# Stick-breaking attention: how the loads of a head are shaped, queued and ordered

## The reference

```python
logits = einsum("bhqd,bhkd->bhqk", q, k) * scale
log_keep = where(visible, log_sigmoid(-logits), 0.0)
log_between = cumsum(log_keep, axis=3, reverse=True) - log_keep
weights = where(visible, exp(log_sigmoid(logits) + log_between), 0.0)
out = einsum("bhqk,bhkd->bhqd", weights, v)
```

## Time and profile before

| | us |
|---|---|
| median of 3 runs | 4376.24 |
| profiled execution, its own time | 4379.16 |
| its span, first to last instruction | 4377.4 |
| PE busy in the span | 4171.0 (95%) |
| DVE busy | 2380.5 (54%) |
| DVE waiting for a gate in the attention, 8 times | 61.2 |

### The profile page before, as it was taken

The page is one execution under the profiler, slowest core; times in us unless marked ns, Lnnn a source line. Parts: engine busy times, 40 slices in busy tenths (PEclk is TensorE's granted clock), DMA queues, the critical chain, the costliest instruction groups (busy, mean ns, idle before and its releaser), DMA issues. The chain is left out here.

```text
span 4377.4 us, 90822 instructions
## 1 busy us (share of the span) xinstructions
PE 4171.0 (95%) x35784; PEld 3344.7 (76%) x35784; DVE 2380.5 (54%) x3103; ACT 1666.2 (38%) x3296; POOL 804.4 (18%) x637
## 2 busy tenths in 40 slices
PE   7999999997999999997999999999899999999999
PEld 7888888985888888885555555655688888878887
DVE  5444444443444444442777777777467766743222
ACT  4222222223222222222666666666444444421111
POOL 2110111111111111110000000000256666610222
PEclk9999999998999999998999999999899999999999
DMA  2333433333333333334443442442233333355653
GB/s 93 109 117 119 122 109 110 102 115 110 109 118 116 109 104 118 107 103 113 89 94 69 82 93 63 87 94 62 75 114 99 101 104 100 92 184 177 189 188 129
DMA packets 486971, 479.74 MB, mean 110 GB/s; under 512 B 260610, under 2 KB 370818, under 8 KB 480914
## 3 DMA queue, kind: packets, MB, share of 16 engines
q1 hardware_dynamic: 475154, 450.33, 37.1%
q10 hardware_dynamic: 11520, 25.17, 1.6%
HBM read 305.45 MB, written 169.93 MB: 109 GB/s over the span
## 5 line engine op out<-in xcount | busy, mean ns | idle before, releaser
L1210 DVE TENSOR_TENSOR_SCAN kept<-keep,kept 128x512 f32<-128x512 f32 (+1 forms) x448 | 436.6, 975 | 63.1 <-ACT keep L1172 22.6
L1172 ACT ACTIVATE keep<-z 128x512 f32<-128x512 f32 (+3 forms) x704 | 343.4, 506 | 302.4 <-PE z L1105 242.1
L1636 POOL TENSOR_TENSOR off<-NT,tri 128x512 f32<-128x512 f32 x165 | 206.1, 1276 | 1181.6 <-ACT NT L1540 1181.6
L1115 PE MATMUL turned<-t_identity,kept 128*128 128x128 f32 (+1 forms) x2432 | 383.0, 280 | 38.6 <-DVE kept L1210 38.6
L1115 PEld LDWEIGHTS turned<-t_identity,kept 128*128 128x128 f32 (+1 forms) x2432 | 280.7, 136 | 154.9 <-DVE kept L1210 50.0
L1182 ACT COPY w<-turned 128x512 f32<-128x512 f32 (+4 forms) x704 | 363.2, 528 | 92.4 <-PE turned L1115 90.7
L1207 DVE TENSOR_TENSOR_SCAN kept<-keep,hidden 128x512 f32<-128x512 f32 (+3 forms) x256 | 284.2, 1116 | 156.3 <-ACT keep L1172 155.7
L1104 PE MATMUL z<-k_high,q_parts 128*128 128x512 f32 (+3 forms) x704 | 308.6, 439 | 36.1 <-DMA k_low<-scr_k_lo 27.9
L1142 PE MATMUL acc<-w,dv 128*64 128x512 f32 (+3 forms) x1280 | 322.8, 562 | 15.4 <-issue 15.4
L1104 PEld LDWEIGHTS z<-k_high,q_parts 128*128 128x128 f32 x704 | 137.8, 196 | 191.5 <-ACT keep L1172 107.6
L1105 PE MATMUL z<-k_low,q_parts 128*128 128x512 f32 (+3 forms) x704 | 256.6, 368 | 0.0
(11 more groups left out here) (554 smaller groups left out, 10688.4 us busy)
## 6 DMA issues: line engine op xcount, KB each, us to landing
w_raw0A<-in_w_main SPq DMA_DIRECT2D x42, 512.0 KB, 3.9
w_raw0B<-in_w_main SPq DMA_DIRECT2D x42, 512.0 KB, 3.9
w_raw1A<-in_w_main SPq DMA_DIRECT2D x41, 512.0 KB, 4.0
w_raw1B<-in_w_main SPq DMA_DIRECT2D x41, 512.0 KB, 3.8
KB<-scr_kb SPq DMA_DIRECT2D x33, 512.0 KB, 5.2
AR<-scr_ar SPq DMA_DIRECT2D x33, 512.0 KB, 5.4
y_raw<-scr_y SPq DMA_DIRECT2D x64, 256.0 KB, 4.5
merge<-scr_merge SPq DMA_DIRECT2D x64, 256.0 KB, 6.3
```

The lines of the kernel that those rows point to most:

```text
L1115: mm = pe.transpose(turned[num % TB][0:size, P * r:P * r + P], kept[kept_in(g)][:, src:src + size], t["identity"][:, :])
L1172: act.activation(keep[num % KB][:, 0:size], z[num % ZB][:, 0:size], ACT.Sigmoid, scale=-DH ** -0.5).then_inc(keep_done, 1)
L1210: dve.tensor_tensor_scan(dst, data, data, kept[kept_in(g)][:, end:end + 1], ALU.mult, ALU.bypass).then_inc(scanned, 1)
L1636: pool.tensor_tensor(out, a, b, op).then_inc(s[name], 1)
```

## The change

Five things are done, all in `attention_phase`.

1. `dv_diag` is loaded over all 128 rows by SP. The edge rows then go into row 127 on top of it, from POOL's queue, after a wait for the landing (`diag_in`, `diag_first`).
2. The load of a head is cut into five kinds (queries, high keys, low keys, steps, diagonal), which `due_after` spreads: odd head: queries at turn 7 of the pair before (for head 1: at turn 0), high keys at turn 0, low keys and steps at turn 1, diagonal at turn 2; even head of the next pair: queries and high keys at turn 3, low keys and steps at turn 4, diagonal at turn 5.
3. The four key loads are issued high, high, low, low instead of high, low, high, low.
4. At the start the constant `hidden` is loaded behind the first part's queries and keys instead of ahead of them, and the first two gates after the first of three parts instead of after the third.
5. PE waits for `v_in` (now 32 for each load) and for the edge rows (`edge_in`, 16).

```diff
+        def due_after(g):
+            pair, turn = divmod(g, 2 * GROUPS)
+            even, odd = 2 * pair + 2, 2 * pair + 1
+            if g == 0:
+                return [(odd, "queries"), (odd, "high")]
+            plan = {0: [(odd, "high")], 1: [(odd, "low"), (odd, "steps")], 2: [(odd, "diagonal")],
+                    3: [(even, "queries"), (even, "high")], 4: [(even, "low"), (even, "steps")], 5: [(even, "diagonal")],
+                    7: [(odd + 2, "queries")]}
+            return [(head, what) for head, what in plan.get(turn, []) if head < HEADS]
...
-            def load(head, first, last, qk_sem, v_sem):
...
-                for part in (low, high):
-                    sp.dma_start(k_high[u][part, ks].bitcast(F32), scratch["k_hi"][rows, src]).then_inc(qk_sem, 16)
-                    sp.dma_start(k_low[u][part, ks].bitcast(F32), scratch["k_lo"][rows, src]).then_inc(qk_sem, 16)
...
-                sp.dma_start(dv_diag[u][0:P - 1, tiles, :], by_tile[0:P - 1, tiles, :]).then_inc(v_sem, 16)
-                sp.dma_start(dv_diag[u][P - 1:P, tiles, :], edge[:, tiles, :]).then_inc(v_sem, 16)
...
+            def load_keys(head, first, last, dst, name, done):
...
+                for part in (slice(0, DH), slice(DH, P)):
+                    sp.dma_start(dst[u][part, ks].bitcast(F32), scratch[name][rows, src]).then_inc(done, 16)
...
+            def load_diagonal(head, first, last, done):
+                u, rows, tiles = head % 2, slice(DH * head, DH * head + DH), slice(first, last)
+                by_tile = scratch["dv"][CHUNK:TOK, rows].rearrange("(k p) c -> p k c", p=P)
+                sp.dma_start(dv_diag[u][:, tiles, :], by_tile[:, tiles, :]).then_inc(done, 16)
...
-            sp.dma_start(hidden[:, :], io["hidden"]).then_inc(const_in, 16)
             for p, (first, last) in enumerate(FIRST_PARTS):
-                load(0, first, last, qk_first[p], v_first[p])
-            load_gate(0)
-            load_gate(1)
+                load_queries(0, first, last, qk_first[p])
+                load_keys(0, first, last, k_high, "k_hi", qk_first[p])
+                load_keys(0, first, last, k_low, "k_lo", qk_first[p])
+                if p == 0:
+                    sp.dma_start(hidden[:, :], io["hidden"]).then_inc(const_in, 16)
+                load_steps(0, first, last, v_first[p])
+                load_diagonal(0, first, last, diag_first[p])
+                if p == 0:
+                    load_gate(0)
+                    load_gate(1)
             for g in range(GROUPS_ALL):
                 sp.wait_ge(y_done, g + 1)
                 store_y(g)
                 if g + 2 < GROUPS_ALL:
                     load_gate(g + 2)
-                if g % (2 * GROUPS) == 0:
-                    head = head_of(g) + 1
-                    load(head, 0, QT, qk_in[head % 2], v_in[head % 2])
-                if g % (2 * GROUPS) == GROUPS - 1 and head_of(g) + 2 < HEADS:
-                    head = head_of(g) + 2
-                    load(head, 0, QT, qk_in[head % 2], v_in[head % 2])
+                for head, what in due_after(g):
...
             def value_steps(g):
                 head = head_of(g)
                 if head == 0:
-                    pe.wait_ge(v_first[min(rank(g), len(FIRST_PARTS) - 1)], 64 if rank(g) == 0 else 48)
+                    pe.wait_ge(v_first[min(rank(g), len(FIRST_PARTS) - 1)], 32 if rank(g) == 0 else 16)
+                    pe.wait_ge(edge_first[min(rank(g), len(FIRST_PARTS) - 1)], 16)
                 else:
-                    pe.wait_ge(v_in[head % 2], 64 * loads_of(head))
+                    pe.wait_ge(v_in[head % 2], 32 * loads_of(head))
+                    pe.wait_ge(edge_in[head % 2], 16 * loads_of(head))
...
+            def load_edges(head, first, last, done):
+                edge = scratch["v_edge"][:, DH * head:DH * head + DH].rearrange("(o k) c -> o k c", o=1)
+                pool.dma_start(dv_diag[head % 2][P - 1:P, first:last, :], edge[:, first:last, :]).then_inc(done, 16)
+
+            for p, (first, last) in enumerate(FIRST_PARTS):
+                pool.wait_ge(diag_first[p], 16)
+                load_edges(0, first, last, edge_first[p])
+            for head in range(1, HEADS):
+                pool.wait_ge(diag_in[head % 2], 16 * ((head + 1) // 2 if head % 2 else head // 2))
+                load_edges(head, 0, QT, edge_in[head % 2])
```

More of the change, by code:

```diff
@@ L987, in attention_phase @@
         qk_first, v_first = [[sem(f"a_{x}_first{b}") for b in range(len(FIRST_PARTS))] for x in ("qk", "v")]
+        edge_first, edge_in = [sem(f"a_edge_first{b}") for b in range(len(FIRST_PARTS))], [sem(f"a_edge_in{b}") for b in range(2)]
+        diag_first, diag_in = [sem(f"a_diag_first{b}") for b in range(len(FIRST_PARTS))], [sem(f"a_diag_in{b}") for b in range(2)]
         qk_in, v_in = [sem(f"a_qk_in{b}") for b in range(2)], [sem(f"a_v_in{b}") for b in range(2)]
@@ L1026, in _, with load_queries @@
         @block.sync
         def _(sp):
-            def load(head, first, last, qk_sem, v_sem):
[L1029 to L1032, removed]
+            def load_queries(head, first, last, done):
+                u, rows, qs = head % 2, slice(DH * head, DH * head + DH), slice(P * first, P * last)
+                sp.dma_start(q_parts[u][0:DH, qs].bitcast(F32), scratch["q_hi"][rows, qs]).then_inc(done, 16)
+                sp.dma_start(q_parts[u][DH:P, qs].bitcast(F32), scratch["q_lo"][rows, qs]).then_inc(done, 16)
@@ L1033, in load @@
+            def load_keys(head, first, last, dst, name, done):
+                u, rows = head % 2, slice(DH * head, DH * head + DH)
                 k0 = P * first + (META if first else 0)
                 ks, src = slice(k0, P * last + META), slice(PAD + k0, PAD + P * last + META)
-                sp.dma_start(q_parts[u][low, qs].bitcast(F32), scratch["q_hi"][rows, qs]).then_inc(qk_sem, 16)
-                sp.dma_start(q_parts[u][high, qs].bitcast(F32), scratch["q_lo"][rows, qs]).then_inc(qk_sem, 16)
@@ L1037, in load, with load_steps @@
-                for part in (low, high):
-                    sp.dma_start(k_high[u][part, ks].bitcast(F32), scratch["k_hi"][rows, src]).then_inc(qk_sem, 16)
-                    sp.dma_start(k_low[u][part, ks].bitcast(F32), scratch["k_lo"][rows, src]).then_inc(qk_sem, 16)
-                tiles = slice(first, last)
+                for part in (slice(0, DH), slice(DH, P)):
+                    sp.dma_start(dst[u][part, ks].bitcast(F32), scratch[name][rows, src]).then_inc(done, 16)
+            def load_steps(head, first, last, done):
+                u, rows, tiles = head % 2, slice(DH * head, DH * head + DH), slice(first, last)
@@ L1041, in load @@
                 by_tile = scratch["dv"][CHUNK:TOK, rows].rearrange("(k p) c -> p k c", p=P)
-                edge = scratch["v_edge"][:, rows].rearrange("(o k) c -> o k c", o=1)
                 if first == 0:
                     sp.wait_ge(cleared, 2)
-                    sp.dma_start(dv[u][0:META, 0, :], scratch["dv"][PAD:CHUNK, rows]).then_inc(v_sem, 16)
-                sp.dma_start(dv[u][:, first + 1:last + 1, :], by_tile[:, tiles, :]).then_inc(v_sem, 16)
-                sp.dma_start(dv_diag[u][0:P - 1, tiles, :], by_tile[0:P - 1, tiles, :]).then_inc(v_sem, 16)
@@ L1048, in load @@
-                sp.dma_start(dv_diag[u][P - 1:P, tiles, :], edge[:, tiles, :]).then_inc(v_sem, 16)
+                    sp.dma_start(dv[u][0:META, 0, :], scratch["dv"][PAD:CHUNK, rows]).then_inc(done, 16)
+                sp.dma_start(dv[u][:, first + 1:last + 1, :], by_tile[:, tiles, :]).then_inc(done, 16)
+            def load_diagonal(head, first, last, done):
+                u, rows, tiles = head % 2, slice(DH * head, DH * head + DH), slice(first, last)
+                by_tile = scratch["dv"][CHUNK:TOK, rows].rearrange("(k p) c -> p k c", p=P)
+                sp.dma_start(dv_diag[u][:, tiles, :], by_tile[:, tiles, :]).then_inc(done, 16)
@@ L1067, in _ @@
                     load_gate(g + 2)
-                if g % (2 * GROUPS) == 0:
-                    head = head_of(g) + 1
-                    load(head, 0, QT, qk_in[head % 2], v_in[head % 2])
-                if g % (2 * GROUPS) == GROUPS - 1 and head_of(g) + 2 < HEADS:
-                    head = head_of(g) + 2
-                    load(head, 0, QT, qk_in[head % 2], v_in[head % 2])
+                for head, what in due_after(g):
+                    qk, v = qk_in[head % 2], v_in[head % 2]
+                    if what == "queries":
+                        load_queries(head, 0, QT, qk)
+                    elif what == "high":
+                        load_keys(head, 0, QT, k_high, "k_hi", qk)
+                    elif what == "low":
+                        load_keys(head, 0, QT, k_low, "k_lo", qk)
+                    elif what == "steps":
+                        load_steps(head, 0, QT, v)
+                    else:
+                        load_diagonal(head, 0, QT, diag_in[head % 2])
             for b in range(2):
```

## The result

The changed kernel takes 4301.76 us, the median of 4 runs (4298.37 to 4304.05), against 4376.98 us before (4 runs). The ratio is 0.9827, 95% interval 0.981 to 0.9844: 1.7% faster. The forecast was 4300. Measured once more with five runs beside two of the experiments it was 4303.18, ratio 0.9832 (0.9818 to 0.9845).

The account below looks back on a forecast made before the run. The prediction took SP, stopped by a diagonal load on one DMA engine, to bound the kernel. Seven stretches (57 us) and the start (20 us) gave 77 us off 4379.2, so 4302, named 4300 against the median; range 4285 to 4328.

Parts of the forecast that it names:

- The bound: Even-head loads: the 127-row diagonal on one DMA engine holds SP some 32 us, so gates and edges come late.
- One sign: In the changed profile of the attention, SP would never be held over 1 us by a DMA issue.
- The seven stretches: Sum 6 to sum 8 in seven head pairs: DVE-bound, 16.9 us instead of 25.04 each, 57 us in all.
- The start: Start of attention: part 1's queries 6.1 us earlier, part 2's 6.81 us wait gone, first gates 7.5; 20.4 us.
- The sum: Whole kernel: 57 + 20 = 77 us off the profiled 4379.2 gives 4302, named as 4300 against the median.
- What was costed at nothing: Even heads: spread loads stay hidden, low keys with 3.2 us to spare; POOL's edges land at 2187.2 against 2192.80.
- the second rival: Even heads' low keys land late: PE waits 2.3 us each, as much again where the clock falls; 4316 to 4332, chance 0.10.
- The first rival: Sum 6 to sum 8: clock stays low after any short gap, gaining only 38 us, start 14; 4324, chance 0.12.
- The third: First product after turn 7: diagonal and edges land late, diagonal on one engine or POOL's DMA starved; 4455, chance 0.05.

Follow-up runs that it names:

- the shape alone: Kernel before with the diagonal over 128 rows and edge rows on POOL, old load places, keys high, high, low, low: 4301.83 us.
- the experiment: Changed kernel with an even head's queries and high keys moved from turn 3 to turn 4, low keys last: 4367.27 us.
- part 1 first: Changed kernel with part 1's queries and keys issued ahead of part 0's steps, diagonal and gates, part 2's ahead of part 1's: 4300.18 us.

## Why the prediction was right

*The bound.* Right as read: SP held behind a diagonal on one DMA engine. The row count as the cause, argued from two loads in the trace, is now shown by the two runs with 112 and 15 rows. What the Trainium skill says of 127 and 128 rows (DMA: Bandwidth & Descriptors, Why a DMA increments its semaphore by 16 and not by 1) agrees with the 4.9 us against over 32, and with a DMA share of 1.03 against 0.08. One sign was missed by a little: single issues of SP in the attention took up to 1.5 us where I had said never over 1; no wait for a gate or for value steps came of it.

*The seven stretches.* I had 16.9 us each and 57 in all; measured 16.9 and 56.9. But the reason was wrong. I called the stretch DVE-bound (15.89 us of work at 94%) and put PE's work at full clock at 15.6. The row of after that stands against the earlier trace rows has PE busy 16.86 of 16.90: PE is the bound there, and DVE has a little room. My figure for PE took all the time at the low clock as busy time. It also left out three matmuls: the row of before counts 97 where after has 100, and the stretch behind it 81 where after has 78, so three of them, 0.76 us (13.85 less 13.09), now fall ahead of sum 8. That makes 16.1 us for the 97, not 15.6. And the clock of 0.87 was that of the first stretch, the highest of the seven; the lowest was 0.73. The right number came out by luck. The run with the multiply on POOL doesn't test this, since it made the scans slower.

*The start.* 20.4 us forecast. Sum 0 came 13.5 us earlier counted from SP's first issue (33.75 against 47.29), for 12.9; sum 0 to sum 1 fell from 22.44 to 14.90, 7.5 as forecast: 21.1 us. Part 1's logits came 5.7 us earlier (6.1), part 2's wait is gone; the wait for part 1 was 4.07 us, not near 3. But the cause of the 7.5 was not the one I gave. In the run with the shape alone the gates are still the last issues of the start, and sum 0 to sum 1 takes 14.91 us as well: with quick diagonals SP comes to the gates in time. The early gates even cost a little there. Without them ahead of part 1, PE waits 1.90 us for it instead of 4.07, and sum 0 comes 1.3 us earlier (32.45 against 33.75). Only with the slow diagonal does their new place bring the 7.5.

*The sum.* 21.1 + 56.9 = 78.0, less 2.3 in the two longer stretches of sums 8 to 9 (16.10 for 14.91, and 16.43 for what was 15.26), gives the 75.7 us measured. That loss was not in my sum: PE now stands 1.8 us in front of DVE's scans there, where it stood 0.9 to 1.3 (the three matmuls that moved ahead of sum 8 are missing there), and in two pairs the clock falls behind it.

*What was costed at nothing.* PE in the changed kernel, at the first logits and at the first product of head 2:

```profile
2151.29 0.33 PE L1134 MATMUL z<-k_high,q_parts 128*128 128x144 f32 x1
...
2169.59 0.87 PE L1172 MATMUL acc<-w,dv 128*64 128x512 f32 x3
```

The second low-key load left at about 2140.5 and lands in 6.4 us, so at 2146.9 against 2151.29: 4.4 us to spare (3.2 forecast). The edges are in at 2162.7 against 2169.59: 6.9 to spare (5.6). So the second rival was close to coming true but did not, and the experiment gives its price: some 8.6 us a pair for a wait of 6.6, less than the doubling that I had put. The first rival, a clock that stays low, did not come: PEclk is 1.00 in all seven stretches. Its premise, a low clock after any short gap, was too broad: between sums 8 and 9 of before PE had gaps of 0.9 to 1.3 us at a clock of 1.00. The third needs a slow diagonal; with one it is 358 us slower than before, far above my 79. I had priced the even heads alone, at 91 us; their stretches from sum 6 to sum 8 cost 153, and the odd heads', from sum 3 to sum 4, another 209. POOL beside DVE's work issued an edge load in 0.5 us, and it landed in 1.8 us (the median of 15), so the starving of POOL's DMAs that the Trainium skill warns of (SBUF — State Buffer, Two separate sides) does not show here; whether any DVE instruction of this kernel runs in one of the fast modes that the warning is about, no run shows. For POOL's computing the same page says that a DVE instruction with two SBUF inputs contends with a POOL one that reads SBUF (Who interferes with whom); the scans' 44.9 us agree with it, and so does the scan of 2.05 us beside a multiply against 1.28.

## What to carry to other kernels

When a queue's issue takes many microseconds, look at the DMA ahead of it, and at the DMA share while it lasts: 0.08 is about one engine of sixteen, and the count of rows of that load is the first suspect. Cut such a load into counts that spread (here 112 and 15) before rearranging the order of loads: three edited places did what the whole change did, and the new order with the old shape lost 358 us. A wait on a busy pipeline costs more than its length: 7.5 us for 5.7, and 60 for 46.

## What the runs showed of the hardware

- The issue of a full load behind another still holds SP: 12.96 us for a diagonal of 128 rows right behind the steps, 0.59 us when a turn lies between them. It did no harm here, since nothing urgent stood behind it.
- The landing of a tiny load hangs on what else moves: the edge rows landed 1.8 us after POOL's issue, and 6.1 us after it where SP issued two gates and 1 MB of queries at the same time.
- POOL's multiply of 64x512 took 2.28 us on average, nearly always beside DVE's scans, and 1.25 us at the end where no scan ran, and the scans grew by 6% (720.9 to 765.8 us).
- After a PE gap of 1.8 us between sums 8 and 9 the clock fell in two of seven pairs of the changed kernel, in one of seven with part 1 first, and in three of seven with the shape alone; in the kernel before, where the same gap is 0.9 to 1.3 us, it fell in none. What decides it among the gaps of 1.8 us stays open and was not tried.
